# Dense operands on a 512-byte grid plus 256, own rows for layer 2, and the mixer's set-up in another order

## The reference

```python
h_res = concatenate([meta, x], axis=1)                      # (1, 528, 1024)
for i in range(2):
    h = rms_norm(h_res, ln_mix[i])
    mix = s5_mixer(h, ...) if i % 2 == 0 else sink_window_attention(h, ...)
    h_res = h_res + mix
    h_res = h_res + swiglu_ffn(rms_norm(h_res, ln_ffn[i]), w_gate[i], w_up[i], w_down[i])
return rms_norm(h_res, ln_f)[:, 16:]
```

## The kernel before

| tensor | before: start, mod 512 | row, bytes | after: start, mod 512 | row, bytes |
|---|---|---|---|---|
| w_high | 49792, 128 | 512 | 50176, 0 | 512 |
| w_low | 57984, 128 | 512 | 58368, 0 | 512 |
| x_high | 178016, 352 | 2112 | 179968, 256 | 2112 |
| x_low | 194912, 352 | 2112 | 197376, 256 | 2112 |
| a_high | 85088, 96 | 2112 | 85760, 256 | 2112 |
| a_low | 131552, 480 | 2112 | 132864, 256 | 2112 |
| glu_high | 85088, 96 | 2112 | 85760, 256 | 2112 |
| glu_low | 101984, 96 | 2112 | 103168, 256 | 2112 |
| o_high | 131456, 384 | 2048 | 132352, 256 | 2048 |
| o_low | 147840, 384 | 2048 | 149248, 256 | 2048 |
| x1_high, x1_low | | | 179968, 256; 196864, 256 | 2048 |
| a1_high, a1_low | | | 85760, 256; 131328, 256 | 2048 |

## Time and profile before

### The profile page before, as it was taken

The page is one execution under the profiler, slowest core; times in us unless marked ns, Lnnn a source line. Parts: engine busy times, 40 slices in busy tenths (PEclk is TensorE's granted clock), DMA queues, the critical chain, the costliest instruction groups (busy, mean ns, idle before and its releaser), DMA issues.

```text
span 1281.6 us, 19892 instructions
## 1 busy us (share of the span) xinstructions
PE 1177.1 (92%) x8035; PEld 1039.0 (81%) x8035; DVE 622.9 (49%) x907; ACT 395.3 (31%) x653; POOL 227.6 (18%) x216
## 2 busy tenths in 40 slices
PE   4257658999999999999999999999999999999997
PEld 4246547999999999999999966658888888888886
DVE  5989993454343433334444344426434334434443
ACT  5311112233322222223333354434322222222322
POOL 3788870000211112110000000000121111110000
PEclk9986777999999999999999999989999999999999
DMA  7212333323223322322323211103222333322222
GB/s 126 70 41 53 68 71 86 98 68 99 91 73 98 98 86 78 98 70 91 90 90 119 84 66 34 34 1 99 83 86 94 98 98 98 98 70 90 90 90 86
DMA packets 119512, 104.57 MB, mean 82 GB/s; under 512 B 21996, under 2 KB 117344, under 8 KB 119136
## 3 DMA queue, kind: packets, MB, share of 16 engines
q1 hardware_dynamic: 109096, 99.58, 26.0%
q10 hardware_dynamic: 10368, 4.33, 1.5%
HBM read 98.11 MB, written 5.24 MB: 81 GB/s over the span
## 4 chain that ended last, share of the span: by engine, by line
issue 42%; PE 40%; DVE 11%; POOL 3%; DMA 1%; SPq 1%; ACT 1%; ACTq 0%; POOLq 0%; DVEq 0%
PE banks L1217 38%; POOL gate L517 2%; DVE zs L1003 1%; DMA raw_c_im<-in_ssm_c_im 1%; DVE zt L1006 1%; DVE z L1001 1%; DVE inj L960 1%; DVE inj L961 1%; DVE inj_t L959 1%; DVE inj_t L962 1%; PE banks L1304 1%; DVE w_low L800 0%; DVE z L1000 0%; DVE inj L958 0%; SPq L350 0%
## 5 line engine op out<-in xcount | busy, mean ns | idle before, releaser
L543 ACT CAST w_high<-raw 128x1024 fp32r<-128x1024 f32 x188 | 197.2, 1049 | 599.5 <-PE banks L1217 599.5
L800 DVE TENSOR_TENSOR w_low<-raw,w_high 128x1024 fp32r<-128x1024 f32 x188 | 230.8, 1228 | 209.2 <-ACT w_high L543 209.2
L1217 PE MATMUL banks<-x_high,w_high 128*128 128x264 f32 (+1 forms) x1184 | 322.7, 325 | 1.1 <-DVE x_low L1033 1.1
L1217 PE MATMUL banks<-x_low,w_high 128*128 128x264 f32 (+1 forms) x1184 | 321.1, 324 | 0.0
L1217 PE MATMUL banks<-x_high,w_low 128*128 128x264 f32 (+1 forms) x1184 | 320.0, 323 | 0.0
L1217 PEld LDWEIGHTS banks<-x_high,w_high 128*128 128x128 f32 x1184 | 197.1, 189 | 21.0 <-issue 1.6
L1217 PEld LDWEIGHTS banks<-x_high,w_low 128*128 128x128 f32 x1184 | 198.1, 189 | 18.3
L1217 PEld LDWEIGHTS banks<-x_low,w_high 128*128 128x128 f32 x1184 | 197.6, 188 | 18.2
L517 POOL TENSOR_TENSOR gate<-gate,rstd_row 128x528 f32<-128x528 f32 (+1 forms) x44 | 79.3, 1803 | 395.2 <-ACT gate L681 395.1
L1217 PE MATMUL banks<-a_high,w_low 128*128 128x264 f32 (+1 forms) x528 | 140.9, 321 | 0.0
L1217 PE MATMUL banks<-a_low,w_high 128*128 128x264 f32 (+1 forms) x528 | 140.8, 321 | 0.0
(11 more groups left out here) (272 smaller groups left out, 1389.3 us busy)
## 6 DMA issues: line engine op xcount, KB each, us to landing
raw<-in_ffn_w_gate SPq DMA_DIRECT2D x22, 1024.0 KB, 5.3
raw<-in_ffn_w_up SPq DMA_DIRECT2D x22, 1024.0 KB, 5.3
raw<-in_ffn_w_down SPq DMA_DIRECT2D x16, 768.0 KB, 4.7
raw<-in_ffn_w_down SPq DMA_DIRECT2D x16, 640.0 KB, 4.4
raw<-in_attn_w_qkv SPq DMA_DIRECT2D x6, 1024.0 KB, 5.2
raw<-in_ssm_w_glu_b SPq DMA_DIRECT2D x4, 1024.0 KB, 5.3
raw<-in_ssm_w_glu_a SPq DMA_DIRECT2D x4, 1024.0 KB, 5.2
k_toep<-k_dram SPq DMA_DIRECT2D x64, 64.0 KB, 3.0
```

The source lines that it names most:

```text
L543: nc.scalar.copy(w_high[:, j], raw[:, slot, :, j * P:(j + 1) * P]).then_inc(w_rounded, 1)
L800: nc.vector.tensor_tensor(w_low[:, j], raw[:, slot, :, j * P:(j + 1) * P], w_high[:, j], ALU.subtract).then_inc(w_split, 1)
L1217: ins = nc.tensor.matmul(banks[:, bank + h, 0:cn], w[:, j, k, :], xx[:, first_k + k, c0 + base:c0 + base + cn], start=start and k == 0 and ...
```

## The change

It has three parts.

1. Addresses. `sb` takes an alignment. w_high and w_low start on a multiple of 512 bytes. Each moving operand is made by `streamed`: a pad of 256 bytes that is itself on a multiple of 512, and the tensor right behind it, so that it starts at 256 past a multiple.
2. Shapes. Layer 2's feed-forward has tensors of its own, x1 and a1, with rows of 512 tokens; they lie over x and a, whose contents are no longer wanted then. The 528 positions are split 256 + 272 in place of 264 + 264; the first part is written to the second half of its PSUM bank, so that the result is one run of 528 across two banks, and the readers (lines 1048, 1080, 1086 and others) take it as one run.
3. The mixer's set-up. SP loads B ahead of the tokens and C after two of their four quarters, with a semaphore for each. TensorE transposes B and C ahead of the tokens. The eight copies into the residual and the four into bbar_pair move from VectorE to ScalarE. VectorE makes all four nat copies first, and powr ahead of the input's mean square and of the fine table. GpSimd makes the coarse table after reads(0), and not before. `additions` waits for u_copied too.

```diff
-        def sb(name, shape, dt=F32, scope=ctx):
-            return scope.enter_context(nc.sbuf_tensor(name, shape, dt))
+        def sb(name, shape, dt=F32, scope=ctx, align=32):
+            return scope.enter_context(nc.sbuf_tensor(name, shape, dt, align_bytes=align))
+
+        def streamed(name, shape, scope=ctx):
+
+            sb(name + "_shift", [P, STREAM_SHIFT // 4], scope=scope, align=STREAM_LINE)
+            return sb(name, shape, F32R, scope=scope)
...
-        w_high = sb("w_high", [P, 2, KB, P], F32R)
+        w_high = sb("w_high", [P, 2, KB, P], F32R, align=STREAM_LINE)
...
-        a_high = sb("a_high", [P, FB, L], F32R)
-        a_low = sb("a_low", [P, FB, L], F32R)
+        short_rows = ExitStack()
+        a1_high = streamed("a1_high", [P, FB, SEQ], scope=short_rows)
+        a1_low = streamed("a1_low", [P, FB, SEQ], scope=short_rows)
+        short_rows.close()
+        a_high = streamed("a_high", [P, FB, L])
+        a_low = streamed("a_low", [P, FB, L])
...
+        short_input = ExitStack()
+        x1_high = streamed("x1_high", [P, KB, SEQ], scope=short_input)
+        x1_low = streamed("x1_low", [P, KB, SEQ], scope=short_input)
+        short_input.close()
+        x_high = streamed("x_high", [P, KB, L])
+        x_low = streamed("x_low", [P, KB, L])
...
-        def halves(n):
-
-            return [(0, HALF), (HALF, HALF)] if n == L else [(META, SEQ)]
+        def parts_of(n):
+
+            return [(0, FIRST, 512 - FIRST), (FIRST, L - FIRST, 0)] if n == L else [(META, SEQ, 0)]
 
         def bank_view(first, n):
 
-            return banks[:, first:first + 2, 0:HALF] if n == L else banks[:, first, 0:SEQ]
+            if n != L:
+                return banks[:, first, 0:SEQ]
+            return banks[:, first:first + 2, :].rearrange("p b c -> p (b c)")[:, 512 - FIRST:512 - FIRST + L]
...
+            for i, (k, w) in enumerate((("b_re", b_re), ("b_im", b_im))):
+                sp.dma_start(braw[k][:], w.rearrange("o (r j) n q -> (o r) (j n q)", j=2)).then_inc(bc_loaded[i], 16)
             for i in range(4):
+                if i == 2:
+                    for n, (k, w) in enumerate((("c_re", c_re), ("c_im", c_im))):
+                        for j in range(2):
+                            sp.dma_start(braw[k][:].rearrange("r (q j n) -> r q j n", q=GROUP, j=2)[:, :, j, :],
+                                         w.rearrange("o (r j) q n -> (o r) j q n", j=2)[:, j]).then_inc(bc_loaded[2 + n], 16)
                 sp.dma_start(xt[META // T:C, 2 * i:2 * i + 2, :], xv[:, 2 * i:2 * i + 2, :]).then_inc(x_loaded[i], 16)
...
+            res_v = residual[:].rearrange("p k (c s) -> p k c s", s=T)
+            for s in range(T):
+                act.wait_ge(res_t, s + 1)
+                b0 = 2 * (s % 2)
+                nc.scalar.copy(res_v[:, :, :, s].rearrange("p (h k) c -> p h k c", h=2),
+                               banks[:, b0:b0 + 2, 0:4 * C].rearrange("p h (k c) -> p h k c", k=4)).then_inc(res_copied, 1)
+
             act.wait_ge(rstd0, 1)
             for i in range(5):
+                if i == 2:
+                    act.wait_ge(nat_ready, 1)
+                    act.wait_ge(pairs_cleared, 1)
+                    for j in range(2):
+                        for h, part in enumerate(("b_re", "b_im")):
+                            ins = nc.scalar.copy(bbar_pair[j * STATE:(j + 1) * STATE, h, :, j * GROUP:(j + 1) * GROUP],
+                                                 nat[part][j * STATE:(j + 1) * STATE])
+                    ins.then_inc(bbar_placed, 1)
...
-                        for h, (c0, cn) in enumerate(parts):
+                        for h, (c0, cn, b0) in enumerate(parts):
                             last_one = k == w_k + nk - 1 and w is w_low
-                            base = 0 if xx is not o_high and xx is not o_low else -META
-                            ins = nc.tensor.matmul(banks[:, bank + h, 0:cn], w[:, j, k, :],
+                            base = -META if xx.shape[2] == SEQ else 0
+                            ins = nc.tensor.matmul(banks[:, bank + h, b0:b0 + cn], w[:, j, k, :],
...
+                pe.wait_ge(bc_loaded[i], 16 if i < 2 else 32)
+                if i == 1:
+                    pe.wait_ge(mag_arg, 1)
...
             def additions(b):
 
                 pe.wait_ge(inj_copied, b + 1)
+                pe.wait_ge(u_copied, b + 1)
```

147 lines of the change are left out of this document (70 added, 77 removed).

## The result

The changed kernel takes 1269.65 us (median, 1269.10 to 1270.49) against 1284.91 for the kernel before on the same chip: ratio 0.9885, 95% interval [0.9872, 0.9899]. The change saves 15 us where 32.6 were forecast, so the prediction was wrong in size; 1269.65 lies just inside its range (1226 to 1270) and near its rival C (1267). The profiled execution took 1269.1 us, its span 1267.2 (before 1284.27 and 1281.6). TensorE's busy time fell by 13.6 us, VectorE's by 12.5.

A forecast was written before the change was run, and what follows sets the result against it. Dense matmuls back to back on TensorE bound the kernel from about 223 us, VectorE in the mixer before. Gains of 9.0 + 0.5 + 14.7 + 8.4 = 32.6 off 1284.3, plus 1.0, gave 1252.7 us; range 1226 to 1270.

The forecast's parts named there:

- rival C: Dense matmuls cost columns plus a fixed piece, only layer 2's 32-byte offset was dear: 1267 us, chance 0.20.
- Part 1: Layer 2's operands moved onto 64-byte edges, 256 from the weights: 232.4 to 226.7 ns for 1584 matmuls, 9.0 us.
- The queries: Attention's 192 query matmuls, long rows now starting on 64-byte edges: half of 1.1 us counted, 0.5 us.
- Part 2: Layer 1 and the mixer's output product, split 256 + 272: one block less in each of 2064 pairs, 14.7 us.
- the block law: Dense matmuls cost 7.1 ns per 64-byte block their moving operand touches; three shapes agreed within 2%.
- 17 and 17 blocks: Layer 1's halves of 1056 bytes touch 17 blocks of 64 bytes at either offset, so they cost alike.
- Part 3: Mixer set-up reordered: first injection at 54.4 not 62.76 us, released by ScalarE's u_state; gain 8.4 us.
- ScalarE's terms behind the residual copies: Set-up: u_row groups, u_state copies, bbar copies and a tail, 20.9 us from 33.5, so u_state is whole at 54.4.
- fine 3.7: Set-up on VectorE: the fine table takes 3.7 us, in the chain that has nat_ready at 40.
- The 8.4 is carried to the dense part: From 68 us on VectorE has no idle time, so the set-up's 8.4 us reaches the dense matmuls whole.
- B: Weights and stream no longer meet with weights on the grid, rate nears the floor: about 1195, halfway 1223, chance 0.15.
- E: Slower: a power-of-two distance makes stream and weights collide in every matmul, +22 us, 1307 us, chance 0.07.

The follow-up runs named there:

- the order repaired: Changed kernel with GpSimd's coarse table ahead of reads(0) again, as before the change: 1269.32 us, ratio 0.9886.
- both repairs: Changed kernel with GpSimd's coarse table ahead of reads(0), 1269.32 us; and, separately, with VectorE's nat_b ahead of its fine table, 1267.17 us.
- the long rows: Changed kernel with layer-1 rows of 2304 bytes, halves 264 + 264, 1258.68 us; the trace meant adds coarse table first and useless matmuls in two TensorE waits, 1256.86 us.
- nat first: Changed kernel with VectorE's scaled input matrices (nat_b) ahead of its fine table: 1267.17 us, ratio 0.9867.
- a twelfth: Trace of the changed kernel with rows of 2304 bytes, halves 264 + 264, and nat_b ahead of VectorE's fine table: 1259.14 us, ratio 0.9793.

## Why the prediction was wrong, step by step

- **Part 1, 9.0 us: right**, in size and place (8.7 from layer 2's input loop to the end; 8.5 for all operands by themselves). The reason was wrong in its wording: not the 64-byte edge, but the distance to the weights. The prediction named both properties of the out-projection's rows and could not tell them apart; the run with the streams at 128 does (10 us back, all edges kept).
- **The queries, 0.5: not seen.** Their distance went through 32, 96, 160 and 224 with k and now goes through 0, 64, 128 and 192, and they take 232.2 ns where they took 232.8, 0.1 us in all; from layer 1's down product to the attention's first output product the difference to before goes from 6.0 to 5.3, not up.
- **Part 2, 14.7 us: the step that failed.** "A pair touches 33 blocks and not 34, 7.1 ns each": the block law was fitted to three rates and agreed within 2% by chance, since 512, 264 and their rates allow many such laws. A bare matmul of 256 columns takes 120.3 ns where its 16 blocks would be 113.6. Measured in the kernel: 121.7 as before in the inputs, 0.8 us worse in the down product, and 122.5 against 121.7 in the mixer's output product (0.6 us). Bare, both splits cost 243 a pair in rows of 2112 bytes. That first and second halves cost alike before, which was taken for 17 and 17 blocks, is what a mean over four distances looks like.
- **Part 3, 8.4 us: mechanism right, size off.** Released by ScalarE, residual copies at 33.45, k_lag behind it: as written (ScalarE's terms behind the residual copies add up to 20.7 us, where the prediction has 20.9). The term that was mis-sized is "fine 3.7": 10.7, since GpSimd's reads(0) now ran beside it. It moved nat_b from 40 to 44.2 (the powers ended 2.3 us and the gains 0.8 under their terms, which hid the rest) and the injection from 54.4 to 57.4. The Trainium skill has this, and I did not use it: by "SBUF — State Buffer", Who interferes with whom, a VectorE instruction with two inputs in SBUF contends with a GpSimd instruction that reads SBUF. The rows agree: 0.28 us alone, 1.19 beside it. One row fits less well: the first slow operation (29.34, 1.15 us) ran for the most part beside GpSimd's MEMSET of k_toep (29.45 to 30.40), which reads nothing, while an operation beside the same MEMSET in the kernel before kept its 0.69 us (at 49.11). The move of GpSimd's reads ahead of its coarse table, counted at nothing, was the cause.
- **"The 8.4 is carried to the dense part": failed too.** With the order repaired (injection 54.1, skip_joins 59.7, as predicted) the end did not move. VectorE's last state row came 8.7 us earlier than before, but of these 6.4 were left at the last glu_low, 5.1 at layer 1's first input product and 3.6 at its loop. The first step is the slow store to y_dram. The other two go with TensorE's clock, which the sum did not look at: around the wait for the last glu_low it was low for 10.3 us (6.8 before), and from 310.9 to 314.3 it was low where the kernel before had 2.4 GHz. The changed kernel shows the same two steps (8.5, 7.5, 6.0 in the table; low from 209.1 to 219.3 and from 308.0 to 311.5); it has 1.7 us more at the last glu_low than at the state row because its last outputs ran at the full clock, which those of the kernel before and of both repairs did not. By taking it away only the low clock in the last outputs was put to the test, in one trace of the long rows; the rest is read from the traces alone.
- **The rivals.** C had the time and its sign (118.4 and 124.9 in a pair), not the law: a matmul's price is not its columns and a constant, since 264 columns cost 120.0 or 122.4 by row length and address. Its 1267 added 8.4 for the set-up, of which 5.7 arrived, so its nearness is in part luck. B was half right: the distance between stream and weights is what counts, but 226.7 is already its best case for 512 columns. What E feared, a distance that is dear in every matmul, exists (233.3 ns); it is 128 or 192, which the change does not use in layer 2. The range (1226 to 1270) held the time at its edge, with less than 0.4 us to spare.

## What to carry to other kernels

Keep the streamed rows of a float32r matmul of 512 columns, every row of them, a multiple of 256 bytes away from its weights, and pad rows to a multiple of 256 bytes rather than cut the columns at another place: 3% on 512 columns, 1.4 to 2% on halves of 264. For other column counts measure first: 256 and 272 columns had their best distance elsewhere. A law fitted to three rates by arithmetic is not a price; with one bare row of 48 matmuls per address it would have been known. When work of one engine is moved, look at what will then run beside it, not only at what it waits for, and expect that of a few us gained ahead of a stretch where TensorE waits some go to its clock. In a row of bare matmuls, look at the granted clock before reading the rate.

## What the runs showed that was not expected

- 512 float32r columns: 226.7 ns at a distance of 0 modulo 256, 228.8 at 64, 233.3 at 128 and 192, 237.8 when both start 4 bytes past the line.
- Under 256 columns a float32r matmul with new weights is hardly cheaper: at the full clock 64 columns take 111 to 112 ns and 192 take 109 to 117, where 256 take 120.3. The row's averages for 128 and 192 (207.5 and 152.7 ns, 9.96 and 7.33 us for 48) are those of the low clock, not of the columns.
- A VectorE operation of 0.28 us took 1.19 beside GpSimd's, and GpSimd's read operations of 1.10 to 1.28 us were hardly longer. Beside VectorE's operations of 0.69 to 0.79 us it was GpSimd's short ones in the coarse table that grew (0.27 us before, 0.77 in the changed kernel, lines 433 and 463), and with nat first both grew.
- Behind waits of 1.19 to 1.73 us TensorE stayed at 2.4 GHz in six traces, behind waits of 1.87 to 1.93 us it ran at 1.2 GHz in five, at the same place of the program: 4.4 or 6.8 to 7.1 us for the same outputs. In a twelfth TensorE had no such wait and was at 1.2 GHz ahead of those outputs, in place of during them.
